# Expert weights of gate and up kept as scaled f16 halves, double-buffered, and token rows gathered in two transfers

## What is computed

```python
def hierarchical_moe(xt, w_gr, b_gr, w_er, b_er, w_g, w_u, w_d):
    g_prob = jax.nn.softmax(xf @ w_gr + b_gr, axis=-1)
    g_p, g_idx = lax.top_k(g_prob, 1)
    ...
    e_val, e_idx = lax.top_k(e_logits, TOP_K)
    gates = g_p * jax.nn.softmax(e_val, axis=-1)
    ...
    def expert_block(args):
        xb, e = args
        return (jax.nn.silu(xb @ w_g[e]) * (xb @ w_u[e])) @ w_d[e]
    ...
    y = ybuf.reshape(n_blocks * MOE_BLK, D_MODEL)[dest] * gate_s[:, None]
    return jax.ops.segment_sum(y, tok_s, num_segments=n_tok)
```

## Time and profile before

| what | us |
|---|---|
| median of 3 runs | 2751.67 (2751.11 to 2752.50) |
| the profiled execution, its own time | 2750.93 |
| its span | 2749.3 |
| PE busy / DVE busy / ACT busy / POOL busy | 2643.6 / 1716.2 / 1391.3 / 798.8 |
| mean granted clock of PE, share of full | 0.987 |

### The profile page before, as it was taken

The page is one execution under the profiler, slowest core; times in us unless marked ns, Lnnn a source line. Parts: engine busy times, 40 slices in busy tenths (PEclk is TensorE's granted clock), DMA queues, the critical chain, the costliest instruction groups (busy, mean ns, idle before and its releaser), DMA issues.

```text
span 2749.3 us, 49924 instructions
## 1 busy us (share of the span) xinstructions
PE 2643.6 (96%) x14252; PEld 1820.9 (66%) x14253; DVE 1716.2 (62%) x3920; ACT 1391.3 (51%) x3046; POOL 798.8 (29%) x825
## 2 busy tenths in 40 slices
PE   4999999999999999996699999999999999999997
PEld 2455555555555555553588888888888888888886
DVE  5677777777777777776454455545655444546633
ACT  7666555565555566553344445445545333435533
POOL 1122323232322222331232333323223323333232
PEclk9999999999999999998799999999999999999999
DMA  8376555556655555656556677667767665667763
GB/s 315 82 166 166 156 160 158 152 157 165 163 152 160 154 156 164 166 138 167 187 169 189 186 236 244 200 196 224 235 186 232 205 183 153 194 180 237 235 181 54
DMA packets 546395, 495.22 MB, mean 180 GB/s; under 512 B 411787, under 2 KB 411948, under 8 KB 545340
## 3 DMA queue, kind: packets, MB, share of 16 engines
q1 hardware_dynamic: 517516, 406.08, 49.2%
q0 software_dynamic: 28848, 88.77, 13.8%
HBM read 309.74 MB, written 87.88 MB: 145 GB/s over the span
## 4 chain that ended last, share of the span: by engine, by line
PE 89%; DVE 3%; DMA 3%; ACT 2%; issue 1%; SPq 1%; POOL 1%; POOLq 0%; DVEq 0%; ACTq 0%
PE psB L1676 15%; PE psA L1676 15%; PE psG L574 11%; PE psF L1676 7%; PE psG L1676 7%; PE psE L574 6%; PE psF L574 6%; PE psD L574 6%; PE psC L574 6%; PE psH L574 3%; PE psC L1684 1%; PE psD L1684 1%; PE psE L1691 1%; DMA xg<-hn_rows,slots 1%; DMA slots<-slot_table 1%
## 5 line engine op out<-in xcount | busy, mean ns | idle before, releaser
L574 PE MATMUL psG<-wi_all,both_xT 128*128 128x512 f16 x1536 | 345.2, 382 | 10.9 <-DMA both_xT<-x 10.9
L574 PEld LDWEIGHTS psG<-wi_all,both_xT 128*128 128x128 f16 x1536 | 148.7, 98 | 188.2 <-DMA both_xT<-x 11.1
L1600 POOL DMA_INDIRECT xg<-hn_rows,slots x80 | 99.2, 1240 | 544.0 <-DMA slots<-slot_table 389.4
L1676 PE MATMUL psB<-up_hi,gT_hi 128*128 128x512 f32 x632 | 254.4, 402 | 0.0
L1676 PE MATMUL psA<-gate_hi,gT_hi 128*128 128x512 f32 x632 | 247.3, 391 | 3.1 <-ACT gT_hi L1796 1.7
L1812 DVE TENSOR_TENSOR down_lo<-wi_all,down_hi 128x512 fp32r<-128x512 f32 x256 | 157.0, 686 | 147.1 <-ACT down_hi L1770 147.1
L1676 PE MATMUL psB<-up_hi,gT_lo 128*128 128x512 f32 x632 | 247.6, 392 | 0.0
L1676 PE MATMUL psA<-gate_hi,gT_lo 128*128 128x512 f32 x632 | 247.3, 391 | 0.0
L1676 PE MATMUL psA<-gate_lo,gT_hi 128*128 128x512 f32 x632 | 247.0, 391 | 0.0
L1676 PE MATMUL psB<-up_lo,gT_hi 128*128 128x512 f32 x632 | 246.4, 390 | 0.0
L1796 ACT ACTIVATE gT_hi<-psC 128x512 fp32r<-128x512 f32 x80 | 47.8, 597 | 384.8 <-PE psC L1684 384.8
(11 more groups left out here) (320 smaller groups left out, 5777.2 us busy)
## 6 DMA issues: line engine op xcount, KB each, us to landing
wi_all<-in_w_gate SPq DMA_DIRECT2D x32, 2048.0 KB, 9.5
wi_all<-in_w_up SPq DMA_DIRECT2D x32, 2048.0 KB, 12.9
wi_all<-in_w_down SPq DMA_DIRECT2D x32, 2048.0 KB, 11.7
xt<-in_x SPq DMA_DIRECT2D x32, 512.0 KB, 3.7
um<-u_rows SPq DMA_DIRECT2D x64, 256.0 KB, 2.7
out_rows<-h SPq DMA_DIRECT2D x32, 512.0 KB, 3.0
xres<-in_x SPq DMA_DIRECT2D x31, 512.0 KB, 4.1
hn_rows<-xres SPq DMA_DIRECT2D x31, 512.0 KB, 2.9
```

The costliest lines, as they stand in the source:

```text
L574: m = nc.tensor.matmul(ps, left[:, l, k, :], weights.half(r, k, n, width), start=(k == opens and j == 0), stop=(k == closes and j == 2))
L1600: pool.indirect_dma_start(xg[:], None, hn_dram, bass.IndirectOffsetOnAxis(ap=slots[:, 0, 0:1], axis=0), bounds_check=SEQ + P - 1).then_inc ...
L1676: m = nc.tensor.matmul(ps[:, :], l[:, k, :], r[:, r_k[n], :], start=(n == 0 and j == 0), stop=(n == len(l_k) - 1 and j == 2))
```

## The change

Five things are done together.

1. The gate and up weights are split into f16 halves instead of fp32r ones, and the transposed rows `gT_hi`/`gT_lo` too; down and its activations stay fp32r. f16 has a narrow range, so gate and up of each expert are multiplied by a power of two of their own before the split, and the results are multiplied back in silu (a scale operand) and in the product (a `scalar_tensor_tensor` in place of a `tensor_tensor`). The rows use the scale `hn_scale` that the router already had.
2. That power of two comes from the largest per-partition sum of absolute values. ACT makes the sums, one pass over 128x4096 per weight (`sum_up`, into a junk tile). For expert 0 POOL takes the maximum over the partitions (`partition_all_reduce`). For the others DVE masks the sums to their exponents and writes two diagonal matrices (`spread_bound`), PE multiplies them by ones into psH (`every_bound`, one matmul of 256 columns), and DVE reduces psH and works out the powers (`scales`, 5 small steps).
3. There are two sets of gate and up halves, and two float32 places for each, so that expert e+1 is split while expert e is multiplied. Splits are two pieces of 128x2048 instead of eight of 128x512, and PE waits for the whole weight in the first block of an expert. The loads of gate and up run two experts ahead.
4. `hn_rows` is kept as two tables of 512 columns; each block is gathered by two indirect transfers, and PE transposes the first half without waiting for the second.
5. `walk` writes blocks 0 and 1 of every expert out and loops over the rest, so each expert has at least 2 blocks (before: at least 1, and 2 for expert 0).

```diff
-    hn_dram = nc.dram_tensor("hn_rows", [SEQ + P, D], F32).ap()
+    hn_dram = [nc.dram_tensor(f"hn_rows_{c}", [SEQ + P, CC], F32).ap() for c in range(2)]
...
+        place = [wi_flat[:, j * 4096:(j + 1) * 4096].rearrange("p (k n) -> p k n", k=8) for j in range(5)]
+        raw = {"gate": (place[0], place[3]), "up": (place[1], place[4]), "down": (place[2], place[2])}
+        raw_in = {n: [keep.enter_context(nc.semaphore(f"raw_in_{n}_{p}")) for p in range(1 if n == "down" else 2)] for n in raw}
...
-            sp.dma_start(hn_dram[bass.ds((t - 1) * P, P), :], places(t)[2][:]).then_inc(hn_out.sem, 16)
+            for c in range(2):
+                sp.dma_start(hn_dram[c][bass.ds((t - 1) * P, P), :], places(t)[2][:, c * CC:(c + 1) * CC]).then_inc(hn_out.sem, 16)
...
-        step(v.tensor_scalar(blocks_of[:, counts], blocks_of[:, E:], 1, None, ALU.max))
-        step(v.tensor_scalar(blocks_of[:, 0:1], blocks_of[:, 0:1], 2, None, ALU.max))
+        step(v.tensor_scalar(blocks_of[:, counts], blocks_of[:, E:], 2, None, ALU.max))
...
-    hi = {n: sb(f"{n}_hi", [P, 8, 512], F32R) for n in raw}
-    lo = {n: sb(f"{n}_lo", [P, 8, 512], F32R) for n in raw}
+    SCALED = ("gate", "up")
+    hi = {n: [sb(f"{n}_hi_{p}", [P, 8, 512], F16) for p in range(2)] for n in SCALED}
+    lo = {n: [sb(f"{n}_lo_{p}", [P, 8, 512], F16) for p in range(2)] for n in SCALED}
+    hi["down"], lo["down"] = ([sb(f"down_{w}", [P, 8, 512], F32R)] * 2 for w in ("hi", "lo"))
...
+        def expert(e, p, r, follow=2):
+            n = eng.value_load(blocks_of[0:1, bass.ds(e, 1)], min_val=2, max_val=TILES)
+            base = eng.value_load(blocks_of[0:1, bass.ds(e + E, 1)], min_val=0, max_val=4 * TILES)
+            start = 0 if isinstance(e, int) and e == 0 else base
+            block(e, 0, start, p, r, follow)
+            block(e, 1, start + 1, p, r, follow)
+            with eng.If(n > 2):
+                with eng.Fori(2, n) as i:
+                    block(e, i, start + i, p, r, follow)
+            return base + n
+        expert(0, 0, 0)
+        with eng.Fori(0, (E - 4) // 2) as pair:
+            expert(pair * 2 + 1, 1, pair)
+            expert(pair * 2 + 2, 0, pair + 1)
+        expert(E - 3, 1, (E - 3) // 2)
+        expert(E - 2, 0, (E - 2) // 2, 1)
+        return expert(E - 1, 1, (E - 1) // 2, 0)
...
+        sp.wait_ge(summed, 2)
+        for n in SCALED:
+            load_expert(sp, n, 1, 1)
         mixed(sp)
-        with sp.Fori(1, E) as e:
-            for n in raw:
-                sp.wait_ge(hi_s[n], 8 * e)
-                sp.wait_ge(lo_s[n], 8 * e)
-                load_expert(sp, n, e)
+        reload("gate", 0, 0, 2)
+        reload("up", 0, 0, 2)
+        with sp.Fori(0, (E - 4) // 2) as pair:
+            next_loads(pair * 2, 0)
+            next_loads(pair * 2 + 1, 1)
+        next_loads(E - 4, 0)
+        reload("down", E - 3, 0, 1)
+        reload("down", E - 2, 0, 1)
...
+            for h in range(2):
+                pool.indirect_dma_start(xg[:, h * CC:(h + 1) * CC], None, hn_dram[h],
+                                        bass.IndirectOffsetOnAxis(ap=slots[:, 0, 0:1], axis=0),
+                                        bounds_check=SEQ + P - 1).then_inc(rows_in[h], 16)
...
+        pool.wait_ge(summed, 2)
+        pool.partition_all_reduce(most(0), sums(0), P, RMAX).then_inc(most_s, 1)
...
+        def every_bound(e):
+            pe.wait_ge(diagonal_s, 2 * e)
+            nc.tensor.matmul(every_row, ones[:, :], diagonal[:, :], start=True, stop=True).then_inc(every_s, 1)
...
+            if first:
+                weights("gate", e)
+            split_mm(psA, range(KD), (gT_hi, gT_lo), (hi["gate"][p], lo["gate"][p]), list(range(KD))).then_inc(gate_ps, 1)
+            if follow and (second if is_zero(e) else first):
+                every_bound(e + 1)
...
+        def sum_up(n, e, p, r, junk):
+            act.wait_ge(raw_in[n][p], 16 * (r + 1))
+            if not (is_zero(e) and n == "gate"):
+                act.wait_ge(summed, 2 * e + of[n])
+            s.activation(junk, raw[n][p].rearrange("p k n -> p (k n)"), ACT.Abs, accum_out=sums(p, n)).then_inc(summed, 1)
+        def split(n, e, p):
+            act.wait_ge(step_s, SCALE_STEPS * (e + 1))
+            for c in range(CHUNKS):
+                s.activation(chunk(hi[n][p], c), chunk(raw[n][p], c), ACT.Copy, scale=power(p, n)).then_inc(hi_s[n], 1)
...
+            if is_zero(e) and first:
+                turn_x(b + 1)
+                sum_up("gate", 1, 1, 0, junk)
+                sum_up("up", 1, 1, 0, junk)
+                split_down(e, b)
+            elif is_zero(e) and second:
+                split("gate", 1, 1)
+                turn_x(b + 1)
+                sum_up("gate", 2, 0, 1, junk)
+                sum_up("up", 2, 0, 1, junk)
+                act.wait_ge(summed, 6)
+                split("up", 1, 1)
+            elif first:
+                if follow:
+                    split("gate", e + 1, 1 - p)
+                turn_x(b + 1)
+                if follow > 1:
+                    sum_up("gate", e + 2, p, r + 1, junk)
+                split_down(e, b)
+            elif second:
+                if follow > 1:
+                    sum_up("up", e + 2, p, r + 1, junk)
+                turn_x(b + 1)
+                if follow > 1:
+                    act.wait_ge(summed, 2 * (e + 3))
+                if follow:
+                    split("up", e + 1, 1 - p)
...
+        def spread_bound(e, p):
+            dve.wait_ge(summed, 2 * (e + 1))
+            hold(dve, held)
+            v.tensor_scalar(most(p).bitcast(I32), sums(p).bitcast(I32), 0x7F800000, None, ALU.bitwise_and).then_inc(masked, 1)
+            dve.wait_ge(masked, e)
+            hold(dve, held)
+            for c in range(2):
+                v.tensor_scalar(diagonal[:, c * P:(c + 1) * P], ident, most(p)[:, c:c + 1], None, ALU.mult).then_inc(diagonal_s, 1)
...
+            if follow and (second if is_zero(e) else first):
+                scales(e + 1, 1 - p)
+            if not (known and b == 0):
+                turn(b)
+            if follow and (second if is_zero(e) else first):
+                split("gate", e + 1, 1 - p)
+            product(b, p)
+            turn_x(b + 1)
+            if first:
+                split_down(e)
+            if is_zero(e) and first:
+                spread_bound(1, 1)
+            if second and follow:
+                split("up", e + 1, 1 - p)
+            if second and follow > 1:
+                spread_bound(e + 2, p)
```

More of the change, by code:

```diff
@@ L1537, in experts @@
         "out table hn_dram cst ident blocks_of held raw raw_in load_expert keep mixed").split())
-    slots, slots_old, rows_of_y = (env[n] for n in ("slots", "slots_old", "rows_of_y"))
-    psA, psB, psC, psD, psE, psF, psG = (env[f"ps{c}"] for c in "ABCDEFG")
+    slots, slots_old, rows_of_y, rt_stat, own, wi_flat = (env[n] for n in (
+        "slots", "slots_old", "rows_of_y", "rt_stat", "own", "wi_flat"))
+    psA, psB, psC, psD, psE, psF, psG, psH = (env[f"ps{c}"] for c in "ABCDEFGH")
     def sb(name, shape, dt=F32):
@@ L1709, in block_ @@
                 pe.wait_ge(silu_s, b)
-            split_mm(psA, range(KD), (gT_hi, gT_lo), (hi["gate"], lo["gate"]), list(range(KD)), first, "gate", e
-                     ).then_inc(gate_ps, 1)
+            if first:
[3 more added lines that the diff above has]
+                every_bound(e + 1)
             if not static0:
                 turn_act(b)
-            split_mm(psB, range(KD), (gT_hi, gT_lo), (hi["up"], lo["up"]), list(range(KD)), first, "up", e
-                     ).then_inc(up_ps, 1)
+            if first:
+                weights("up", e)
+            split_mm(psB, range(KD), (gT_hi, gT_lo), (hi["up"][p], lo["up"][p]), list(range(KD))).then_inc(up_ps, 1)
             transpose_rows(b + 1)
             if not static0:
-                loaded = 8 * e if first else 8 * (e + 1)
-                pe.wait_ge(hi_s["down"], loaded)
-                pe.wait_ge(lo_s["down"], loaded)
+                if second:
+                    weights("down", e)
                 down(b)
@@ L1782, in silu @@
                 act.wait_ge(act_s, b)
-            s.activation(gated[:], psA[:, :], ACT.Silu).then_inc(silu_s, 1)
+            s.activation(gated[:], psA[:, :], ACT.Silu, scale=inverse(p, "gate")).then_inc(silu_s, 1)
         def turn(b):
@@ L1796, in turn_x, with block_ @@
                 s.activation(gT_hi[:, 4 * h:4 * h + 4, :].rearrange("p k c -> p (k c)"), ps[:, :],
-                             ACT.Copy).then_inc(xgT_hi, 1)
+                             ACT.Copy, scale=hn_scale).then_inc(xgT_hi, 1)
+        def block_(e, i, b, p, r, follow):
+            known = isinstance(b, int)
+            first, second = isinstance(i, int) and i == 0, isinstance(i, int) and i == 1
+            junk = hi["up"][1 - p][:].rearrange("p k n -> p (k n)").bitcast(BF16)
+            if not (known and b < 2):
+                copy_y(b)
+            if not (known and b == 0):
```

(31 more changed lines are left out.)

209 lines of the change are left out of this document (114 added, 95 removed).

## The result

| | before | after |
|---|---|---|
| median of the runs, us | 2751.61 | 2806.82 (2804.32 to 2812.63) |
| ratio | 1 | 1.0203, 95% interval 1.0186 to 1.0221 |
| profiled execution: time, span | 1.6 us above its span of 2749.3 | 2812.63, span 2811.0 |

What follows compares the result with a forecast made beforehand. PE was taken to be bound by its own matmuls (89% of the span). f16 -40.0, bound matmuls +3.3 and stage change +17.0 gave -19.7 us: span 2729.6, median 2732 us, range 2720 to 2752.

Steps and rivals of the forecast that it cites:

- No block added: Expert blocks: no expert has fewer than two of the 79 blocks, so the new minimum of two costs nothing.
- f16, -40.0 us: Gate and up on PE: f16 matmuls save 0.52 us a block over 77 blocks, -40.0 us.
- The bound's matmul: Each expert after the first, on PE: one matmul of 256 columns, 0.11 us, 30 times, +3.3 us, without waiting.
- ACT and DVE hidden: Expert stage: ACT's extra 7.6 us per expert and DVE's 2048-column pieces stay off the path, DVE with 1.1 us spare.
- rival 2: An expert's first block: DVE late with `gT_lo` if pieces take over 2.95 us; 2766 us at 3.5 us; chance 0.08.
- 3.0 us spare. Hidden: POOL in an expert's second block: the second gather costs 1.2 us of issue and gap, leaving 3.0 us spare.
- rival 1: Second gather in each expert's second block: rows come late; at 1.2 us per expert 2769 us; chance 0.12.
- The mixer, 0: Mixer: one more store issue per tile on SP, which is off the chain there, costs 0.
- (a): Stage change: ACT's two passes end at 1316.6, then POOL takes the maximum before going on, +0.8 us.
- (b): Stage change: two more 2 MB loads slow the first slots request, +3.9 us; the second gather adds +1.2.
- (c): Stage change, block 1: PE stands at the bound's matmul until DVE has written the diagonals, +9.1 us.
- (d): Stage change: the clock falls to 0.50 again after the stop of 9 us, +2.7 us.

Runs made afterwards that it cites:

- slots ahead: The changed kernel with each block's slots read one block ahead, an expert's first block's into a place of its own: 2734.73 us, ratio 0.9935.
- two gathers in before: The kernel before with only the second transfer added (two tables of 512 columns, two stores per tile, two gathers per block): 2782.67 us, ratio 1.0109.

## Why the prediction was wrong, point by point

- **No block added:** held, 79 blocks in both.
- **f16, -40.0 us:** held in size, 0.54 us a block (17.70 to 17.16 without a bound). It shows in the time only once the rows come in time: *slots ahead* takes 1392.4 us from block 0 to the end, where the forecast had 1393.9.
- **The bound's matmul:** 0.11 us, and after expert 1's it waits nowhere. Held.
- **ACT and DVE hidden:** held. The passes take 3.6 + 0.2 us (forecast 3.8), the pieces 2.35 (forecast 2.39). The only wait of psA for `gT_lo` is at the start, so rival 2 did not come.
- **POOL, "3.0 us spare. Hidden": this is the step that failed.** I charged the second gather with its issue alone (1.2 us) and took the spare from one second block with the other durations left as they were. That block was a lucky one, in an expert of three blocks, where the rows land 4.3 us behind the issue. In 9 of the 73 blocks of the kernel before between 1400 and 2700 us they land 9.1 to 9.8 us behind it and less than 0.3 us ahead of PE's demand; in the others the spare is 3.0 us or more. Here is one of the nine, first the gather and then PE's weight load, which waits for it. (A load of the next gate goes out at 1614.46, half a microsecond behind the gather.)

```profile
1613.99 1.19 POOL L1600 DMA_INDIRECT xg<-hn_rows,slots  x1 [7.60 <-DMA slots<-slot_table]
```

```profile
1623.17 0.42 PEld L1684 LDWEIGHTS psC<-cst,xg 128*128 128x128 f32 x4 [0.40 <-DMA xg<-hn_rows,slots]
```

So the spare that counted was nothing, and the second gather alone makes PE wait in 9 blocks (*two gathers in before*). In the changed kernel nine of the 13 stops in that stretch come one block behind those nine. Three durations moved with the change besides. The stretch of both issues went from 1.25 to 3.26 us, not to 2.45. At the place shown the rows land 7.85 us behind the last issue and 10.3 behind the first, and the scatter no longer covers that. And the slots copies and the gathers' issues are held by pieces of 2.35 us, where pieces of 0.69 us stood (the lower half of gate before and after, from 1400 to 2700 us: count, us, mean ns, idle before). I had named all of this under rival 1, with the 4551 ns copy and the Trainium skill's rule on it, and priced it at 1.2 us per expert with a chance of 0.12. I had also read that copy as a rare one, from a median of 202 ns; the mean of 1671 says that it was common. Rival 1 costs (1466.9 - 1392.4)/31 = 2.4 us per expert, unevenly, in 14 blocks. 49 us are waits. Most of the other 25 is the lower clock behind each wait, which I had charged only to the one stop at the start; at the place shown it costs 1.8 us (1.00 and 4.01 us instead of 0.44 and 2.74), and 14 times that is about 26, an estimate.

```profile
L1812 DVE TENSOR_TENSOR gate_lo<-wi_all,gate_hi 128x512 fp32r<-128x512 f32 x240 | 147.2, 686 | 45.0 <-ACT gate_hi L1770 45.0
```

```profile
L1947 DVE SCALAR_TENSOR_TENSOR gate_lo<-wi_all,own,gate_hi 128x2048 f16<-128x2048 f32 x58 | 133.8, 2350 | 39.0 <-ACT gate_hi L1815 39.0
```

On the hold: the Trainium skill's page "SBUF — State Buffer", section "SBUF: two separate sides", says that a VectorE operation with two SBUF inputs and a GpSimd operation that reads SBUF exclude each other for a whole instruction. The runs agree that they do: 2.10 us for a copy of 0.19 beside a piece of 2.35, 191 ns on average once the pieces have 256 columns. They do not agree that one instruction is the limit: in the kernel before, and in *two gathers in before*, GpSimd got no turn between eight short pieces, and a copy took 4.55 us and an issue 5.11. A rule that the trace agrees with in the main, and that bears on an edit which makes those instructions more than three times as long, deserved more than a tail.
- **The mixer, 0:** not settled. The last list is issued at 1316.98 against 1312.38. But over the profiled executions it lies between 1312.4 and 1318.1 with one store per tile and between 1313.4 and 1317.0 with two, so the 4.6 us are within what executions differ by.
- **The start, (a) and (b):** list to block 0 is 27.1 us, forecast 23.3. The slots' landing of 5.28 us was in the sum. That the gather would land in the same traffic was not: 8.85 us after the second issue, where I had left 4.66. The stop (c) is 8.1 us (forecast 9.1). For its clock (d) I had 2.7 us; the transposes and the up matmuls behind it take 0.85 and 6.29 us instead of 0.44 and 5.18, so it costs 1.5.

```profile
1324.34 0.37 POOL L1709 PARTITION_ALL_REDUCE own<-own  x1 [6.38 <-issue]
1324.59 0.74 POOL L1691 DMA_DIRECT2D slots<-slot_table  x1
1330.77 1.29 POOL L1653 DMA_INDIRECT xg<-hn_rows,slots  x1 [5.44 <-DMA slots<-slot_table]
1332.37 1.83 POOL L1653 DMA_INDIRECT xg<-hn_rows,slots  x1 [0.31 <-issue]
```

- **The rule of the Trainium skill's page "TensorE: Matmul & The Clock Gate", section "Back-to-back issue gap"** (about 131 ns): gate and up run at 5.18/24 = 216 ns a matmul here as well, so it did not come.
- **The range** ended at 2752. Rival 1 at 1.2 us per expert was already at 2769, outside it.

## What to carry to other kernels

A serial loop of small steps on a side engine, with two transfer landings in it, has to be added up for a whole turn and compared with the time of a block, under load: a spare read at one place says little, because the smallest one over all blocks decides, and less still when the change moves several of the steps. Near that threshold the causes do not add, and here three cures each brought everything back alone; the one that leaves no work out is to take a landing out of the loop by asking one turn earlier. And a wait of the main engine costs more than its length: here about half as much again in slower matmuls behind it.

## What the runs showed of the hardware that I had not expected

- VectorE's piece length reaches GpSimd's issuing of gathers as well as its copies: an issue takes 1043 ns on average beside pieces of 256 columns, 1267 beside 512 and 1474 beside 2048.
- Short pieces did not help where they followed each other without a gap. In *two gathers in before* the issue of a second gather took 5.11 us beside eight pieces of 512 columns:

```profile
1659.39 5.11 POOL L1602 DMA_INDIRECT xg<-hn_rows,slots  x1 [0.30 <-issue]
```

```profile
1658.71 4.90 DVE L1817 TENSOR_TENSOR up_lo<-wi_all,up_hi 128x512 fp32r<-128x512 f32 x8
```

- Two gathers of 2 KB rows in place of one of 4 KB cost 31 us in a kernel that had none of the other changes, and nothing in the changed kernel once the slots are read ahead.
- Moving two 2 MB loads behind the first gather, together with the other way to the bound, brought block 0 forward by 10.3 us. The slots then land in 2.2 instead of 5.7 us, and the rows about 4.6 us after the gather's issue instead of 8.4.
